# Second layer: twelve late projection halves one per head, second modulation at the last four heads

## The reference

```
h = rms_norm(x, norm1_g[l]) * (1.0 + scale1) + shift1
q, k, v = jnp.split(h @ w_in, 3, axis=-1)          # 16 heads of 64
z = jnp.einsum('bqhd,bkhd->bhqk', q[:, i0:i1], k[:, :i1]) * scale
log_keep = jnp.where(mask, jax.nn.log_sigmoid(-z), 0.0)
later = lax.cumsum(log_keep, axis=3, reverse=True) - log_keep
a = jnp.where(mask, jnp.exp(jax.nn.log_sigmoid(z) + later), 0.0)
x = x + gate1 * (o @ w_out)                        # o: a @ v of all heads
h = rms_norm(x, norm2_g[l]) * (1.0 + scale2) + shift2
x = x + gate2 * hier_moe(h, ...)                   # 32 experts, two per token
```

## Time and profile before

| what | us |
|---|---|
| three timed runs | 1322.48, 1326.14, 1326.82 (median 1326.14) |
| the profiled execution | 1321.83 |
| its span, first to last instruction | 1320.1 |
| the rest of its time, outside the span | 1.7 |
| DMA over the span | 489.98 MB, 371 GB/s on average |
| PE busy | 926.5 (70% of the span) |

### The profile page before, as it was taken

One profiled execution on the slowest core, in us unless ns is written; L12 is line 12 of the kernel. 1 busy time (PEld: TensorE's weight loads), 2 busy tenths in 40 slices (PEclk: granted clock), 3 DMA queues, 4 the chain that ended last, 5 costly groups with the idle time before them and its releaser, 6 DMA issues.

```text
span 1320.1 us, 13677 instructions
## 1 busy us (share of the span) xinstructions
PE 926.5 (70%) x5668; PEld 427.8 (32%) x5668; DVE 262.8 (20%) x573; ACT 203.5 (15%) x423; POOL 30.2 (2%) x89
## 2 busy tenths in 40 slices
PE   4999899557564746556779998985473655655575
PEld 1444555122221212122247664542121212212131
DVE  0545544011010101001020357421010100101011
ACT  2213414010110101000010354330010101000000
POOL 3000000000000000000000022000000000000000
PEclk9999999788787869788889998997786977877898
DMA  9984638999999999999999437499999999999995
GB/s 355 392 260 191 271 143 333 407 428 428 428 428 428 428 429 428 428 427 427 421 408 391 161 142 315 188 388 428 428 428 429 429 428 428 429 428 427 428 424 237
DMA packets 67575, 489.98 MB, mean 371 GB/s; under 512 B 18240, under 2 KB 18368, under 8 KB 37576
## 3 DMA queue, kind: packets, MB, share of 16 engines
q1 hardware_dynamic: 64512, 487.95, 89.4%
q10 hardware_dynamic: 3016, 1.37, 0.4%
HBM read 488.25 MB, written 1.05 MB: 371 GB/s over the span
## 4 chain that ended last, share of the span: by engine, by line
DMA 50%; PE 41%; DVE 4%; SPq 2%; issue 2%; ACT 1%; DVEq 0%
DMA tokens<-in_moe_w_dram 40%; PE bank L881 10%; PE bank L642 9%; DMA ring<-in_moe_w_dram 6%; PE bank L910 6%; PE bank L682 4%; PE bank L794 4%; DMA ring<-in_mod_w_dram 4%; PE bank L607 2%; SPq L400 2%; PE bank L734 1%; ACT att L1080 1%; PE bank L750 1%; PE bank L844 1%; PE bank L919 1%
## 5 line engine op out<-in xcount | busy, mean ns | idle before, releaser
L881 PE MATMUL bank<-ring,region 128*32 128x512 f32 x1472 | 257.8, 664 | 168.9 <-DMA ring<-in_moe_w_dram 82.5
L910 PE MATMUL bank<-ring,region 128*32 128x512 f32 x832 | 149.2, 747 | 149.4 <-DMA ring<-in_moe_w_dram 96.0
L881 PEld LDWEIGHTS bank<-ring,region 128*32 128x32 f32 x1472 | 69.2, 121 | 342.8 <-issue 277.8
L881 PE MATMUL bank<-work,region 128*32 128x512 f32 x256 | 129.4, 664 | 0.0
L881 PE MATMUL bank<-tokens,region 128*32 128x512 f32 x256 | 129.4, 664 | 0.0
L910 PEld LDWEIGHTS bank<-ring,region 128*32 128x32 f32 x832 | 39.4, 133 | 246.9 <-issue 212.4
L642 PE MATMUL bank<-ring,tokens 128*128 128x512 f32 x256 | 115.6, 603 | 2.7 <-ACT tokens L1080 2.7
L1671 DVE TENSOR_TENSOR region<-region,bank 128x512 f32<-128x512 f32 x16 | 11.0, 687 | 433.5 <-PE bank L881 433.5
L1080 ACT ACTIVATE region<-bank,shift,scale 128x128 f32<-128x128 f32 x64 | 24.0, 456 | 380.2 <-PE bank L868 380.2
L1678 DVE TENSOR_TENSOR region<-bank,region 128x512 f32<-128x512 f32 x32 | 20.6, 686 | 289.1 <-PE bank L910 289.1
L868 PE MATMUL bank<-region,h 128*128 128x128 f32 x512 | 63.4, 285 | 9.1 <-issue 8.3
(11 more groups left out here) (232 smaller groups left out, 864.0 us busy)
## 6 DMA issues: line engine op xcount, KB each, us to landing
ring<-in_moe_w_dram SPq DMA_DIRECT2D x144, 2048.0 KB, 19.4
ring<-in_mod_w_dram SPq DMA_DIRECT2D x23, 2048.0 KB, 12.4
work<-in_moe_w_dram SPq DMA_DIRECT2D x22, 2048.0 KB, 24.3
tokens<-in_moe_w_dram SPq DMA_DIRECT2D x22, 2048.0 KB, 28.7
ring<-in_ev_w_in_dram SPq DMA_DIRECT2D x6, 2048.0 KB, 22.5
ring<-in_od_w_in_dram SPq DMA_DIRECT2D x6, 2048.0 KB, 20.2
alone<-in_moe_w_dram SPq DMA_DIRECT2D x2, 2048.0 KB, 11.9
ring<-in_ev_w_out_dram SPq DMA_DIRECT2D x2, 2048.0 KB, 7.8
```

Of the source, the lines that this page charges most:

```text
L881: last = pe.matmul(bank[which][32 * j:32 * j + 32, :], m.seated[:, k, 32 * j:32 * j + 32], weights(4 * which + j, k * FE), start=(k == 0), ...
L910: last = pe.matmul(bank[half][32 * j:32 * j + 32, :], m.hidT[:, c, 32 * j:32 * j + 32], w, start=(c == 0), stop=(c == FC - 1), skip_group_ ...
```

## The change

In the second layer only, three tables of numbers change. The late halves go one per step over steps 0 to 11 instead of over steps 0 to 9 with two halves at steps 0 and 3. The four units of the second modulation go to steps 12 to 15 instead of 10 to 13. `mod_part` on DVE comes after head 15 instead of 14, `mod_cols` on PE at step 16 instead of 15. No instruction is added or taken away.

```
-              {0: [(6, 0), (6, 1)], 1: [(7, 0)], 2: [(7, 1)], 3: [(8, 0), (8, 1)], 4: [(9, 0)], 5: [(9, 1)],
-               6: [(10, 0)], 7: [(10, 1)], 8: [(11, 0)], 9: [(11, 1)]}]
+              {step: [(6 + step // 2, step % 2)] for step in range(12)}]
...
-SECOND_AT = (8, 10)
+SECOND_AT = (8, 12)
...
-SECOND_PART_AT = (14, 14)
-SECOND_COLS_AT = (15, 15)
+SECOND_PART_AT = (14, 15)
+SECOND_COLS_AT = (15, 16)
```

## The result

The changed kernel takes 1329.64 us (median of 20 runs, 1323.37 to 1332.92), the kernel before 1325.26 in 20 runs beside it (1321.38 to 1329.75). The ratio is 1.0028, interval 1.0016 to 1.0039: 2.1 to 5.2 us slower, 3.7 in the middle. A second set, 12 runs of the changed kernel, gave 1.0041 (1.0027 to 1.0055), and the two intervals overlap. Forecast were +2.5 us, 1328.6, and with a chance of 0.75 a difference within 0.3%. The first set lies in it by its middle; both intervals are clear of no change, and the middle of the second set is outside 0.3%.

What follows compares the result with a forecast made beforehand. PE's chain through second-layer attention was taken to bound the time. Pair lengths summed to 100.52 us against 101.24 (-0.7), plus 3.2 for a clock fall: +2.5 on 1326.14 gives 1328.6 us, range 1322.5 to 1333.0.

Steps and rivals of the forecast that it cites:

- The bound: Second layer's attention, 734 to 879 us: one chain through PE; a microsecond won or lost there is one of the total.
- The transfers rule: Rival, whole kernel: DMA is busy most of the time, so the change has no effect, 1326.1 us; chance 0.1.
- ahead of step 2: PE's idle of 1.35 us between steps 1 and 2 stays although one half leaves steps 0 and 1.
- steps 2 and 3: Three halves become two; two heads' chain sets the length, 9.54 us, with some 1.4 idle.
- ACT's copy: Step 8's scores wait until ACT has copied item 9, complete only at the end of step 7: 0.64 us.
- the filled pairs: Steps 8, 9 and 10, 11 carry two halves each and take 9.88 us per pair.
- the addition: At step 16 PE's third output quarter waits for DVE's first addition, queued behind the column operations: 1.37 us.
- The rival that ACT's copies would stretch steps 8 to 11: ACT's copy lies on the path each time, steps 8 to 11 exceed 9.88: +1.3 us on any case; chance 0.05.
- steps 12 and 13: With the first two modulation units at full clock, the heads' chain sets the length: 10.56 us.
- the idle ahead of step 14: PE idles 2.64 us ahead of step 14's scores, the former 2.72 moved there.
- The clock: Falls to half at step 14 for some 7 us after the idle, price 3.2 us; first fall alone chance 0.45.
- the rival's second fall: Another clock fall at step 16, behind small matmuls and a wait: +4.2 to +5.9 us with the first; chance 0.2.

Runs made afterwards that it cites:

- w3_all_filled: Kernel before with gate rows first, halves over steps 0 to 10, modulation at 11, 12, 13, 13, ACT's copies behind the odd head's Ln: 1316.78 us, ratio 0.9953.
- e4_filled_pairs: Kernel before with both halves of item 6 at step 0, one half at steps 1 to 10, modulation at steps 11, 12, 13, 13: ratio 1.0045.
- w1_three_units_early: Changed kernel with the first two output additions ahead of DVE's column operations and modulation at steps 12, 13, 13, 14: ratio to kernel before 0.9986.
- e1_adds_first: Changed kernel with the first two output additions ahead of the three column operations on DVE: ratio to kernel before 1.000.
- g3_adds_and_filler: Changed kernel with the first two additions ahead of DVE's column operations and eight extra matmuls at step 13: ratio to kernel before 1.0003.
- f1_modulation_alone: Kernel before with only the modulation moved to steps 12 to 15, late halves as before: ratio 1.0041.
- e2_filler_after: Changed kernel with eight extra identity matmuls on PE at step 13, ahead of step 14's scores: ratio to kernel before 1.0003.

## Why the prediction was right
**The bound** held for the attention. From the release of the first expert unit to the end the kernel takes 440.7 us in both profiles of the kernel before and 441.1 and 440.8 in the two of the changed one. What PE loses in attention is lost at the end; `w3_all_filled` shows it for a gain too. The transfers rule would have left all ratios at 1.000. The runs disagree: 0.9953 and 1.0045 came from the order of instructions alone, with the same loads. One limit showed: in `e4_filled_pairs` and `w1_three_units_early` the part behind the stretch was 1.2 us shorter than before (42.85), and the last stretch was that much longer (441.9 and 442.2), so that this gain did not reach the end.

**The waits** came out close for most terms: 1.35 forecast and 1.36 found ahead of step 2, 9.54 and 9.54 for steps 2 and 3, 0.64 and 0.68 for ACT's copy, 9.88 and 9.87 for the filled pairs, 1.37 and 1.49 for the addition. The rival that ACT's copies would stretch steps 8 to 11 did not come. The largest error is steps 12 and 13: 10.07, not 10.56, and so the idle ahead of step 14 was 1.98, not 2.64. That term came from the kernel before in its low-clock pair, where POOL's mask fell on head 13's DVE work. First two rows of before, then two of the changed kernel:

```profile
807.83 1.00 POOL L514 TENSOR_TENSOR att<-att,strict 128x384 f32<-128x384 f32 x1 [3.46 <-ACT att L1080]
808.19 1.06 DVE L1531 TENSOR_TENSOR work<-work,att 128x384 f32<-128x384 f32 x1
...
807.06 1.00 POOL L513 TENSOR_TENSOR att<-att,strict 128x384 f32<-128x384 f32 x1 [2.63 <-ACT att L1079]
808.25 0.56 DVE L1530 TENSOR_TENSOR work<-work,att 128x384 f32<-128x384 f32 x1
```

Where the two operations lie side by side DVE's takes 1.06, where POOL's has ended 0.56. The sum at full clock was 100.52, and 102.12 less about 1.6 for the spell is 100.5. That this agrees to 0.1 us is luck: 0.49 too much for steps 12 and 13 stood against 0.16 too little for steps 0 and 1 (a half takes up 3.44 of the pair, not 3.6), 0.15 for steps 6 and 7, and 0.2 from step 14 on, of which 0.12 is the wait of 1.49.

**The clock** was right in kind and place, and its size was wrong: 3.2 us were priced for one spell of 6.9 us at step 14, and 3.4 us at low clock came, costing 1.6: from step 14 on `e1_adds_first` takes 29.62 with the spell and `g3_adds_and_filler` 27.99 without, and the changed kernel takes 31.08 with it against 29.52 in `f1_modulation_alone`, which has none there. In the other profile of the changed kernel the rival's second fall came at step 16 as well, another 1.6, and in `e2_filler_after` it came alone. So the forecast stretch of 103.7 us was met exactly by the second profile (103.72), but by two short spells instead of a long one. That is luck. Idle time before it does belong to the fall at step 14: three of three profiles with 1.98 us fell, none of two with the filler. But the length of it doesn't decide alone, as the 2.86 us of `e4_filled_pairs` show.

**The total**: the two profiles give +0.9 and +2.4 us by the stretch, the runs +3.7 (2.1 to 5.2). Behind the stretch, up to the first expert unit, instructions are the same, yet the time was 45.67 and 45.63 us in the changed kernel and 44.07 and 44.06 in the one before. It goes with the length of the low-clock spell at the router (6.9 us in the former, 3.4 in the latter), and over all kernels it came out near 42.85, 44.07 or 45.65 with a spell of 0, 3.4 or 6.9. (In `e2_filler_after` it was 45.78 with two spells of 3.4.) With these 1.6 us the sums are +2.5 and +4.0, and from the start of step 0 to the end of the span the two profiles differ from the kernel before's by +2.9 and +4.1; both meet the runs. The forecast had put all of this part at nothing (the change "touches nothing outside 734 to 835 us"). Its total of +2.5 was therefore partly luck: -0.7 + 3.2 was forecast, and what came was -0.7, one or two falls of 1.6 each and 1.6 behind the stretch. The longer spell stands in eight of the fourteen profiles (as two short ones in `e2_filler_after`), among them all six of kernels with the modulation at steps 12 to 15, and two of the other eight. That speaks for a link with the change, but no run tests it, and how it would come about isn't shown.

## What to carry to other kernels
Where two engines take turns in pairs, a pair's length is the larger of one engine's work and the other's chain: write down both for each pair, and move work from the end (where nothing waits for the chain) into the pairs with idle time. Moving filler out of one short pair only moves its idle time. Check what each moved step does to the order on the other engines: here the step at which an item ends decided, through ACT's strict order, whether a pair took 9.9 or 11.2 us. And keep small work and waits apart: 1.1 us of tiny matmuls ahead of a 1.5 us wait cost the wait and, in two of four profiles, the clock behind it.

## What the hardware showed that was not expected
Idle times of 2 us (1.98 and 1.99) were followed by spells at half clock of 3.4 us in the changed kernel, 2.72 us by 6.9 us in both profiles of the kernel before, 4.92 us by 10.2 us in `f1_modulation_alone`, and 2.86 us in `e4_filled_pairs` by none. A spell started at the wait of step 16 in one of the changed kernel's two profiles and not in the other, with waits equal to 0.01 us. With eight extra matmuls (1.95 us) in the idle time the clock stayed up there in all three kernels that had them (one profile each), at no cost to the pair (10.07 us with and without).
